# GpSimd makes the low parts in front of the first gates, which start behind 22 chunks; a gap of 7 before the last phase; earlier quarter stores

## The reference, cut to what matters

```python
def peer_ffn(h, wq, sub_keys, u, v):              # 16384 experts, 8 heads, 16 chosen per head
    q = einsum('td,de->te', xc, wq)               # queries
    s = einsum('thpd,hpnd->thpn', q, sub_keys)    # two sets of 128 keys per head
    sv, si = top_k(s, 16)
    cand = sv[:, :, 0, :, None] + sv[:, :, 1, None, :]
    cidx = si[:, :, 0, :, None] * 128 + si[:, :, 1, None, :]
    top, pos = top_k(cand, 16)
    eidx = take_along_axis(cidx, pos)             # expert numbers
    g = softmax(top)
    a = gelu(einsum('thkd,td->thk', u[eidx], xc))
    return einsum('thk,thkd->td', g * a, v[eidx])
```

## Time and profile before

| | us |
|---|---|
| median of 3 runs (lowest, highest) | 1521.2 (1520.54, 1522.17) |
| the profiled execution | 1523.7 |
| its span, first to last instruction | 1521.9 |
| PE busy | 1485.8 (98%) |
| DVE busy | 1270.7 (83%) |
| ACT busy | 713.5 (47%) |
| POOL busy | 621.2 (41%) |

### The profile page before, as it was taken

One profiled execution on the slowest core, in us unless ns is written; L12 is line 12 of the kernel. 1 busy time (PEld: TensorE's weight loads), 2 busy tenths in 40 slices (PEclk: granted clock), 3 DMA queues, 4 the chain that ended last, 5 costly groups with the idle time before them and its releaser, 6 DMA issues.

```text
span 1521.9 us, 24327 instructions
## 1 busy us (share of the span) xinstructions
PE 1485.8 (98%) x8276; PEld 1325.0 (87%) x8276; DVE 1270.7 (83%) x2491; ACT 713.5 (47%) x1411; POOL 621.2 (41%) x511
## 2 busy tenths in 40 slices
PE   5999999999999999999999999999999999999998
PEld 4887777888999999999989999999999988888886
DVE  6788665689999989898678888888999988888876
ACT  4444553233345747576554344444444444443344
POOL 1121300033461424253356555556767655555301
PEclk9999999999999999999999999999999999999999
DMA  9854320122355879899999999999999999999962
GB/s 360 296 175 155 144 79 1 40 100 90 106 186 181 281 230 297 276 300 301 318 362 378 354 359 355 364 339 369 396 385 389 369 371 411 383 380 391 346 243 104
DMA packets 164147, 417.14 MB, mean 274 GB/s; under 512 B 12745, under 2 KB 70217, under 8 KB 163921
## 3 DMA queue, kind: packets, MB, share of 16 engines
q1 hardware_dynamic: 95984, 244.88, 45.1%
q0 software_dynamic: 41472, 151.01, 26.3%
q10 hardware_dynamic: 26594, 20.05, 4.1%
HBM read 376.57 MB, written 38.80 MB: 273 GB/s over the span
## 4 chain that ended last, share of the span: by engine, by line
PE 79%; DVE 13%; DMA 3%; issue 1%; SPq 1%; ACT 1%; POOL 0%; ACTq 0%; DVEq 0%; POOLq 0%
PE bank_S L1092 17%; PE bank_O L1030 14%; PE bank_T L1092 11%; PE bank_S L1030 9%; PE bank_G L1092 6%; PE bank_T L1070 5%; PE bank_O L773 2%; DMA u_raw<-in_u_t 2%; PE bank_S L740 2%; DVE mod_acc L2294 2%; DVE mod_acc L2264 2%; DVE v_sb L2270 1%; DVE v_sb L2257 1%; DVE si L2276 1%; DVE si L2263 1%
## 5 line engine op out<-in xcount | busy, mean ns | idle before, releaser
L1725 ACT ACTIVATE v_hi<-v_raw 128x1024 fp32r<-128x1024 f32 x124 | 131.5, 1061 | 284.6 <-PE bank_G L1092 272.2
L1694 ACT ACTIVATE u_hi<-u_raw 128x1024 fp32r<-128x1024 f32 x128 | 135.4, 1058 | 207.8 <-PE bank_O L1030 104.9
L2575 DVE TENSOR_TENSOR v_lo<-v_raw,v_hi 128x1024 fp32r<-128x1024 f32 x124 | 152.1, 1227 | 86.6 <-ACT v_hi L1725 63.4
L1430 POOL DMA_INDIRECT row<-in_peer_v,stage x128 | 176.4, 1378 | 42.2 <-issue 38.1
L1030 PE MATMUL bank_S<-h_hi,u_hi 128*128 128x352 f32 x576 | 191.7, 335 | 1.4 <-ACT a_act L1745 1.3
L1430 POOL DMA_INDIRECT row<-in_peer_u,stage x128 | 145.4, 1136 | 103.9 <-POOL stage L1426 98.2
L1030 PE MATMUL bank_S<-h_lo,u_hi 128*128 128x352 f32 x576 | 184.9, 323 | 0.0
L2565 DVE SCALAR_TENSOR_TENSOR y<-row,wgt,y 128x1024 f32<-128x1024 f32 x128 | 164.2, 1283 | 0.0
L2591 DVE SCALAR_TENSOR_TENSOR row<-row,h 128x1024 f32<-128x1024 f32 x128 | 156.2, 1221 | 0.0
L1030 PE MATMUL bank_O<-h_lo,u_hi 128*128 128x352 f32 x448 | 144.7, 325 | 0.0
L1030 PE MATMUL bank_O<-h_hi,u_hi 128*128 128x352 f32 x448 | 143.8, 322 | 0.0
(11 more groups left out here) (450 smaller groups left out, 3773.1 us busy)
## 6 DMA issues: line engine op xcount, KB each, us to landing
u_raw<-in_u_t SPq DMA_DIRECT2D x128, 512.0 KB
v_raw<-in_peer_v SPq DMA_DIRECT2D x128, 512.0 KB
g_in<-gates SPq DMA_DIRECT2D x32, 768.0 KB
ada_late<-in_w_ada SPq DMA_DIRECT2D x8, 2048.0 KB, 8.4
gates<-g_out SPq DMA_DIRECT2D x8, 2048.0 KB, 10.1
spill<-a_act ACTq DMA_DIRECT2D x64, 176.0 KB
a_act<-spill SPq DMA_DIRECT2D x16, 704.0 KB
w_raw<-in_w_in SPq DMA_DIRECT2D x20, 512.0 KB, 4.0
```

The lines of the kernel that those rows point to most:

```text
L1430: pool.indirect_dma_start(rows[slot][:, :], None, table[:, :], bass.IndirectOffsetOnAxis(stage[:, place:place + 1], 0))\
L1694: act.activation(u_hi[c % 2][:, :], u_raw[:, c % 2, :], ACT.Copy).then_inc(s_uhi, 1)
L1725: act.activation(v_hi_end[:, i % TAIL, :] if end else v_hi[:, c % 2, :], v_raw[c % 4][:, :], ACT.Copy)\
L2575: dve.tensor_tensor(lo[:, q, :], v_raw[c % 4][:, :], hi[:, q, :].bitcast(f32), ALU.subtract)\
```

## The change

The first gap shrinks from 23 chunks to 22 and the fourth grows from 6 to 7: phases 0, 1 and 2 begin one chunk earlier, and the gap in front of the x block is one chunk longer, so the x block stays at chunks 64 and 65. POOL makes every low part of the first gap (15 to 21 move to it from DVE; 22, now beside the first block, is POOL's too). `FIRST_LOW` goes. ACT's conversions begin behind chunk 11 and the exponent stands behind chunk 15. The x dots of the gaps move one chunk earlier with their phases. The quarters of a phase's last block are issued earlier: in a gap of 7 behind chunks 0, 1, 3 and 4 of it (before: 1, 3, 5, 6), in a gap of 6 two behind chunk 0, then 2 and 3 (before: 1, 2, 4, 5). Beside the x block POOL makes chunk 66's low part before it waits for, and issues, the first row's gather.

```diff
-GAPS = [23, 7, 6, 6]
+GAPS = [22, 7, 6, 7]
...
-FIRST_LOW = 15
-LOW_ON_POOL = set(range(FIRST_LOW)) | {i for p, blocks in enumerate(PHASES)
+LOW_ON_POOL = set(BETWEEN[0]) | {i for p, blocks in enumerate(PHASES)
                                        for i in range(BESIDE[blocks[0]], BETWEEN[p + 1].start + 1)}
-DOTS_AFTER = {30: 1, 31: 1, 32: 1, 45: 1, 46: 1, 47: 1, 58: 3, 59: 2, 60: 2}
+DOTS_AFTER = {29: 1, 30: 1, 31: 1, 44: 1, 45: 1, 46: 1, 57: 3, 58: 2, 59: 2}
...
-        GATES_AT, NUMBERS_AT = FIRST_LOW + 2, FIRST_LOW - 3
+        GATES_AT, NUMBERS_AT = 15, 11
...
-            for i in range(FIRST_LOW):
+            for i in BETWEEN[0]:
                 split_u(i, i)
...
                     if blocks[-1] == X_BLOCK:
+                        split_u(i, i)
                         if i == BETWEEN[phase + 1].start:
                             pool.wait_ge(s_xdot, XN)
                             pool.wait_ge(s_idx, NT)
                             gather(0, 0)
-                        split_u(i, i)
...
-                    while stored < 4 and (stored + 1) * len(gap) <= 4 * (n + 1):
+                    while blocks[-1] != X_BLOCK and stored < 4 and (stored + 1) * len(gap) <= 4 * (n + 3):
                         store_quarter(blocks[-1], stored)
...
-                split_u(FIRST_LOW)
...
-                split_u(FIRST_LOW + 1)
...
-                split_u(FIRST_LOW + 2)
...
                 if phase == 0:
-                    first = FIRST_LOW + 3
-                    decode(NT - 1, s_dv, [([first], [], [first + 1]), ([], [first + 2], [])])
-                    split_and_dot(first + 3)
+                    decode(NT - 1, s_dv, [([], [], []), ([], [], [])])
                     normalise()
-                    split_and_dot(first + 4)
...
-                    rest = list(range(first + 5, BETWEEN[0].stop))
+                    rest = []
...
                     if phase == len(PHASES) - 1:
-                        for n in rest[0:2]:
+                        ahead = len(rest) - 3
+                        for n in rest[0:ahead]:
                             split_and_dot(n)
-                        rest = rest[2:]
+                        rest = rest[ahead:]
```

## The result

| | before, us | after, us |
|---|---|---|
| median of 6 runs each (lowest, highest) | 1521.2 (1520.2, 1522.2) | 1531.8 (1530.7, 1533.5) |
| the profiled execution | 1523.7 | 1532.3 |
| its span | 1521.9 | 1530.4 |
| waits of PE from 404 us to the main loop | 6.4 | 16.5 |

What follows compares the result with a forecast made beforehand. PE, busy 98%, bounds the kernel, so only its waits or slower work count. 10.95 + 2.7 − 1.2 + 0.6 − 0.4 − 0.7 = 11.95 on 1523.7 gives 1535.6; less 2.5 for the median, 1533.1; range 1526.2 to 1537.2.

Steps and rivals of the forecast that it cites:

- POOL's low part holds DVE: Decode before the first gates: two-input DVE instructions stand still while POOL's low part runs, 2.40 us against DVE's 1.14.
- rivals of moments: First gates' decode: POOL holds DVE only for moments, X under 5.9, faster, 1516.9 us; chance 0.09.
- half: First gates' decode: POOL is more often the one waiting, X 8.5, 1523.8 to 1526.5 us; chance 0.09.
- X = 15.1: First gates' decode: DVE blocked 15.1 us in all, from walking low parts 15 to 21 through it at POOL's pace.
- the bounds: DVE's blocked time: 12.2 us if double-rate single-input instructions pass, 15.4 if plain shifts and the reduction are held too.
- PE resumes at 494.84: First gates: PE resumes 0.14 us behind gates ready at 494.7, instead of at 487.73, 7.1 us later.
- 3.84 us for the chunk: First gates: one chunk less lies behind PE and comes back only in the last gap, 3.84 us more.
- Clock, 2.7: Behind the first gates' wait: 14 us of PE idle lowers the clock; 5.4 us at half speed lose 2.7 us.
- the rival that it doesn't: First gates' wait: the idle doesn't lower the clock, +9.25 us, 1530.4 us; chance 0.22.
- Stores −1.2 and +0.6: Hot-row waits before phase 2 (0.8) and the last phase (0.4) go; stores beside u loads give 0.6 us back.
- Last gap −0.4 and −0.7: Last gap: the 0.4 us wait for `gate` goes; the 1.4 us wait before the main loop shrinks by 0.7.
- rival of 0.07: Later gaps: sooner stores and the longer gap do nothing, 1.7 us more, 1534.8 us; chance 0.07.

Runs made afterwards that it cites:

- experiment 1: The changed kernel with low parts 15 to 21 given back to DVE: 1526.5 us, ratio 1.0027.
- alone in 2: The kernel before with only low parts 15 to 22 moved from DVE to POOL: 1533.4 us, ratio 1.0063.
- by itself in 3: The kernel before plus unused POOL scratch-row operations per high part 15 to 21, three runs: subtractions 1534.0 us, copies 1527.3, memsets 1523.9.
- the memsets: The kernel before plus three POOL memsets of a scratch row for each high part 15 to 21: 1523.9 us, ratio 1.0011.
- the subtractions: The kernel before plus one POOL subtraction on a scratch row for each high part 15 to 21: 1534.0 us, ratio 1.0073.

## Why the prediction was right, and where its sizes were off

The sign, the mechanism and the place were right, and the median of 1531.8 lies within 1.3 us of the forecast, inside its range. That it lies so close is luck, for two errors cancel in part. The sum of 11.95 us stands against 8.6 between the profiled executions, 3.4 too large. Against that, the step from the profile to the median took off 2.5 us, as far as the profiled execution of before lay above its median, where that of after lies 0.5 above: 2.0 too much. Inside the sum too the first gates were put 4.6 us too late and the later stretch 1.3 us too early. By its own steps:

- *POOL's low part holds DVE.* Shown: undone in experiment 1, alone in 2, by itself in 3. The rivals of moments and of half (X, the prediction's word for DVE's blocked time, under 5.9 and 8.5) fall with X measured at 12.9.
- *X = 15.1.* The mis-sized term, 2.2 too large. The walk let each low part cost its whole 2.4 us from the end of the DVE instruction then running, and it cost 2.0 to 2.1 (1.5 us over five of them). The two records overlap at both ends: the held instruction of 463.90, at its usual 0.43, must have started at 465.99, 0.14 us before POOL's end at 466.13; and low part 21 found 0.92 us of a DVE instruction still to run and grew by 0.72 only. The scratch operations hold by about 0.3 us less than their own time too (1.5 to 1.7 us of 1.89). And low part 15 lay at 456.0 and not at 457.6, so it covered 0.4 us of the decode and not 1.1. (By the walk's own rule low part 16, from 461.44 on, would have had 0.6 us of shifts and cost 1.8, not 2.1.) The choice between the bounds was right: casts and scalar operations are held too. That the plain shifts pass was taken over untested. The rows speak against it: low part 16 took 2.61 us where it began during one, and a memset held one.
- *PE resumes at 494.84.* Measured 491.61: 2.2 from X, and 1.0 because this execution's decode began at 457.93 and not at 458.94. A likely reason lies in code that the change doesn't touch: behind waits of PE of 0.96 us at most the granted clock fell in the one execution and not in the other (busy time by stage, before and then after):

```profile
226.00:230.00 4.00, 4.00 (x19) 3.04 (x20) 2.58 (x8) 1.90 (x8) 0.00 (x0) 0.57 0.01 4
```

```profile
226.00:230.00 4.00, 3.45 (x23) 2.83 (x23) 3.35 (x11) 2.71 (x10) 0.00 (x0) 1.00 0.00 0
```

  In the six executions that have this fall the decode began at 458.7 to 459.4, in the five that don't at 457.7 to 458.8 (three more, whose clock was also back sooner near 40 us, are left out). No run tests it.

- *3.84 us for the chunk.* Right: phase 2 begins 4.7 us late (649.83 and 654.51) and the last 7.5, 2.8 more, and PE waits 1.2 us less between the two. Experiment 1 shows what the prediction didn't spell out: even with DVE left alone the gates come no sooner, because DVE's work sets them. A chunk less in front of them is then a longer wait, nothing else.
- *Clock, 2.7.* It fell, as forecast, and the rival that it doesn't falls; the size was 1.3. At the low clock the chunk's matmuls begin 0.29 us apart and not 0.16 (492.58 and 492.87), but only until 494.6, 3.0 us of work, and not 5.4 us as at the start of the kernel. And the prediction's evidence for the rival, 7.9 us of idle that "left it at 1.00", was misread. The clock's records in this trace begin at 31.6 us, and a stretch without records is printed as 1.00. PE's own rows show that it ran slow on both sides of that idle stretch already (before):

```profile
7.33 3.54 PE L611 MATMUL bank_G<-c_silu,ada_first 128*128 128x1 f32 x16 [7.33 <-DVE c_silu L1931]
...
18.78 3.57 PE L611 MATMUL bank_G<-ones,mod_acc 128*128 128x1 f32 x16 [7.90 <-DVE mod_acc L1980]
...
33.69 1.03 PE L611 MATMUL bank_O<-ones,sh_acc 128*128 128x1 f32 x8
```

  Sixteen begin 0.21 us apart at 7.33 and at 18.78, eight of the same shape 0.11 apart at 33.69, where the record says 1.00. So the idle stretch says nothing against a fall, and the 0.22 for that rival had nothing to stand on.
- *Stores −1.2 and +0.6.* −0.6 in front of phase 2 as named, but at the last phase +0.7 and not −0.4: the late u load stands in front of the hot rows, where a store did.
- *Last gap −0.4 and −0.7.* The wait for the gate product did not go (0.47 for 0.40), the one in front of the main loop shrank from 1.40 to 1.11. DVE's decode of the last gap is paced by late u loads, not by its x dots: it waits 1.13 and 1.95 us for high parts, for which ACT had waited 5.22 and 2.83 us for loads. The later stretch as a whole gave 0.4 us (9.0 late at the gates, 8.6 at the main loop), and not the 1.7 forecast. That is the rival of 0.07, in substance.

## What to carry to other kernels

Before work goes from DVE to POOL, look at what DVE does while POOL would run. If it reads SBUF with two inputs there, casts or does scalar operations, the price is nearly POOL's time (here 2.1 of 2.4 us) against a saving of 1.14 for DVE, and the balance is minus 1 us an operation, though POOL stood idle. Start a consumer sooner only if its producer will be ready sooner: here the gates came no sooner, and the chunk moved behind them was a loss. And where PE is the bound, count a wait like the ones here of 2.8 us and more as that and 1.3 to 2.6 us of slow clock behind it. Where the clock is read from a view, compare the distance of equal matmuls before a 1.00 is believed.

## What was not expected of the hardware

From 404 us on the clock went by the length of the wait: in all fourteen traces every PE wait of 2.80 us or more saw it at 0.50, during the wait or within 0.5 us behind it (the shortest are 2.80 beside the memsets and 2.90 beside the subtractions, both for low part 15), and none of 2.40 us or less did. Plain transposes held it up as long as they ran. But a long wait isn't needed: near 223 to 226 us it fell to 0.50 in eight of the fourteen (before: 226.2, behind waits of 0.40, 0.96 and 0.23 us), with no wait over 0.97 us in the 8 us before, and that part of the program is the same in all. The price behind a wait differed by a factor of two, 2.6 us behind a wait of 3.3 and 1.3 behind one of 12.8, by how long the slow stretch lasted into PE's work. And a memset, which has no input, still held a cast of DVE from 0.69 to 1.40 us.
